# One norm inside a fused four-block kernel: held weight parts, reordered tile work, and row sums moved from TensorE to GpSimd

## The reference, cut to what matters

```
h = h + rms_norm(mlp_out, norm_ffn_post)            # first model, its last step
sh_m, sc_m, g_m, sh_f, sc_f, g_f = split(silu(c) @ ada_w + ada_b, 6)
h = rms_norm(x, mix_norm) * (1 + sc_m) + sh_m
u = h @ w_in                                        # 5 chunks of 512: a_b, a_c, a_x, r_gate, r_x
y_a = a_b * conv(a_c * a_x);  xr = conv(r_x) + b
y_b = gelu(r_gate) * rg_lru(xr)                     # two gates from xr, then a scan
x = x + g_m * (concat(y_a, y_b) @ w_out)
hf = rms_norm(x, ffn_norm) * (1 + sc_f) + sh_f      # then the SwiGLU, times g_f
```

## Time and profile before

| | |
|---|---|
| Median of 3 runs | 873.94 us (873.6 to 875.2) |
| The profiled execution's own time | 873.45 us |
| Its span, first to last instruction | 871.6 us |
| TensorE busy | 865.7 us, 99% of the span |
| VectorE, ScalarE, GpSimd busy | 714.4, 492.2, 102.3 us |
| Norm and entry in the chain (from the last down matmul to the first of unit U_WIN+2) | 293.37 to 309.93 us |

### The profile page before, as it was taken

One profiled execution on the slowest core, in us unless ns is written; L12 is line 12 of the kernel. 1 busy time (PEld: TensorE's weight loads), 2 busy tenths in 40 slices (PEclk: granted clock), 3 DMA queues, 4 the chain that ended last, 5 costly groups with the idle time before them and its releaser, 6 DMA issues.

```text
span 871.6 us, 13244 instructions
## 1 busy us (share of the span) xinstructions
PE 865.7 (99%) x4801; PEld 739.4 (85%) x4801; DVE 714.4 (82%) x740; ACT 492.2 (56%) x670; POOL 102.3 (12%) x68
## 2 busy tenths in 40 slices
PE   9999999999999999999999999999999999999998
PEld 6998878888888799988888888878777988888887
DVE  6699989898998987998989899787897866655656
ACT  5545665555555757765555455555676555545542
POOL 6000100021120003017010411003000001100000
PEclk9999999999999999999999999999999999999999
DMA  7988669898899385547989798636434376666662
GB/s 253 346 283 315 209 221 333 334 360 331 324 345 340 114 274 186 182 139 216 398 306 333 259 359 298 195 121 216 142 102 152 124 228 182 187 195 189 191 194 72
DMA packets 117252, 208.07 MB, mean 239 GB/s; under 512 B 7259, under 2 KB 81355, under 8 KB 112086
## 3 DMA queue, kind: packets, MB, share of 16 engines
q1 hardware_dynamic: 116710, 205.31, 69.2%
q10 hardware_dynamic: 304, 2.10, 0.7%
q0 software_dynamic: 192, 0.05, 0.0%
HBM read 206.39 MB, written 1.05 MB: 238 GB/s over the span
## 4 chain that ended last, share of the span: by engine, by line
PE 94%; DVE 3%; ACT 1%; DMA 1%; issue 0%; POOL 0%; DVEq 0%; POOLq 0%
PE tp L2033 11%; PE ub L2033 11%; PE acc L1887 8%; PE acc L1890 8%; PE acc L1892 7%; PE tp L2035 6%; PE ub L2035 6%; PE acc L1848 5%; PE acc L1852 5%; PE acc L1851 5%; PE acc L2019 3%; PE acc L2021 3%; PE acc L2020 3%; DVE w_lo L1203 1%; PE tp L2100 1%; PE acc L2100 1%
## 5 line engine op out<-in xcount | busy, mean ns | idle before, releaser
L1203 DVE TENSOR_TENSOR w_lo<-w_raw,w_hi 128x1024 fp32r<-128x1024 f32 x270 | 342.7, 1286 | 77.3 <-ACT w_hi L758 76.8
L758 ACT ACTIVATE w_hi<-w_raw 128x1024 fp32r<-128x1024 f32 x270 | 282.6, 1056 | 196.6 <-PE acc L1892 45.8
L2033 PE MATMUL tp<-aT,w_hi 128*128 128x512 f32 x432 | 135.9, 396 | 0.0
L2033 PE MATMUL ub<-aT,w_hi 128*128 128x512 f32 x432 | 135.4, 395 | 0.0
L1887 PE MATMUL acc<-w_hi,hT_hi 128*128 128x512 f32 x266 | 103.8, 390 | 0.1
L1890 PE MATMUL acc<-w_lo,hT_hi 128*128 128x512 f32 x266 | 103.6, 390 | 0.0
L1892 PE MATMUL acc<-w_hi,hT_lo 128*128 128x512 f32 x262 | 102.0, 389 | 0.0
L2035 PEld LDWEIGHTS tp<-aT,w_lo 128*128 128x128 f32 x432 | 81.1, 188 | 19.2
L2035 PEld LDWEIGHTS ub<-aT,w_lo 128*128 128x128 f32 x432 | 81.1, 188 | 18.9
L666 POOL PARTITION_ALL_REDUCE mod<-mod x14 | 56.4, 4028 | 262.4 <-PE tp L2035 118.7
L2035 PE MATMUL tp<-aT,w_lo 128*128 128x256 f32 x432 | 84.9, 278 | 0.0
(11 more groups left out here) (341 smaller groups left out, 1422.1 us busy)
## 6 DMA issues: line engine op xcount, KB each, us to landing
ada_raw<-in_l_ada_w SPq DMA_DIRECT2D x24, 1024.0 KB, 6.5
w_raw<-in_l_ffn_w_gate SPq DMA_DIRECT2D x44, 512.0 KB, 4.6
w_raw<-in_l_ffn_w_up SPq DMA_DIRECT2D x44, 512.0 KB, 4.4
w_raw<-in_l_ffn_w_down SPq DMA_DIRECT2D x44, 512.0 KB, 3.7
w_raw<-in_w_up SPq DMA_DIRECT2D x32, 512.0 KB, 4.8
w_raw<-in_w_down SPq DMA_DIRECT2D x32, 512.0 KB, 5.6
scratch<-in_l_ada_w SPq DMA_DIRECT2D x14, 1024.0 KB, 7.5
w_raw<-in_attn_w_qkv SPq DMA_DIRECT2D x24, 512.0 KB, 7.3
```

The source lines that it names most:

```text
L758: act.activation(rounded_part(v), w_raw[:, v % SLOTS, :], ACT.Copy).then_inc(hi_done, 1)
L1203: dve.tensor_tensor(rest_part(v), w_raw[:, v % SLOTS, :], rounded_part(v).bitcast(F32), ALU.subtract).then_inc(lo_done, 1)
L2033: pe.matmul(banks[f], rounded_part(v)[:, c[f]], aT[:, :, b, :], start=b == 0, stop=False)
```

## The change

Of the down projection's last parts M0, M1 and M2 go to homes in `hold` and M3 to the upper half of `aT`; before, only M1 lay apart. Therefore token tile 1 of all four is left over until tile 0 is complete (`down_last` with `left=(0, 1)`). The chain of tile 1 goes first on VectorE (its residual ahead of tile 0's remainder), its transposes get banks of their own, and W2 and W3 are rounded by ScalarE earlier, between the squares of tile 0. The four sums by TensorE and the four copies by ScalarE go away; GpSimd now makes six reduces while the recurrent block begins, each released by the remainder of a part (W3, W7, twice W9, twice W13). The loads of two gains move ahead of the MLP's loop.

```diff
-        apart = {2 * (U_WIN - 2) + 1: (flat(aT_hi[:, 4:KB, :]), flat(aT_lo[:, 4:KB, :]))}
+        MLP_END = 2 * (U_WIN - 2)
+        apart = {MLP_END + 3: (flat(aT_hi[:, 4:KB, :]), flat(aT_lo[:, 4:KB, :]))}
...
+        held.update({MLP_END + n: n for n in range(3)})
...
-            if k == 2:
-                return [tp[:, 0, :], tp[:, 1, :]]
+            if k == 2 and t:
+                return [ub[:, 1, :], acc[:, 2, :]]
...
             mlp_slice(1)
+            sp.wait_ge(xn_done, 8)
+            sp.wait_ge(mix_used, 16)
+            load_gain(4)
+            load_gain(5)
             with sp.Fori(0, (NJ_MLP - 2) // 2) as i:
...
             pool.wait_ge(ada_used, 22)
-            partition_sums(G_F, G_F, w_used, parts_to(U_WIN + 5), 2)
+
+            def sum_behind(u, row, n):
+
+                c = row[:, n * CH:(n + 1) * CH]
+                partition_sums(c, c, lo_done, hi_count(2 * u + 1), 0)
+
+            sum_behind(U_WIN + 1, GATE_M, 0)
+            sum_behind(U_WIN + 3, G_F, 0)
+            sum_behind(U_WIN + 4, GATE_M, 1)
+            sum_behind(U_WIN + 4, SH_F, 0)
+            sum_behind(U_WIN + 6, G_F, 1)
+            sum_behind(U_WIN + 6, SH_F, 1)
...
                 half_rstd(0, 1, 5)
+                split_part(2 * u + 2)
                 act.wait_ge(x_half, 3)
...
                 half_rstd(0, 1, 6)
+                split_part(2 * u + 3)
+                act.wait_ge(post_scaled, 5)
+                half_square(1, 0, acc[:, 2, :], sq_half)
                 act.wait_ge(w_used, parts_to(u))
-                half_square(1, 1, acc[:, 3, :], sq_half)
-                act.wait_ge(post_scaled, 5)
-                half_square(1, 0, acc[:, 2, :], sq_done)
-                half_rstd(1, 0, 7)
+                half_square(1, 1, acc[:, 3, :], sq_done)
+                half_rstd(1, 1, 7)
                 norm_hi(2, 0)
-                split_part(2 * u + 2)
-                split_part(2 * u + 3)
...
-                ada_parts(4, 6)
                 norm_hi(2, 1)
-                ada_parts(6, 8)
...
-                dve.wait_ge(sq_half, 7)
+                dve.wait_ge(sq_done, n_rstd[0] + 1)
                 scaled(1, 1, g_post).then_inc(post_scaled, 1)
+                residual(1)
                 norm_lo(0, 0)
-                residual(1)
-                norm_lo(0, 1)
                 dve.wait_ge(norm_scaled, 2)
                 norm_rows(1, g, shift)
+                norm_lo(0, 1)
...
-                    ada_gain(0, 4, pool_sum, 6)
+                    ada_gain(0, 4, pool_sum, 9)
...
-            down(U_WIN - 2, 0, operand=last_h, left=(1,))
-            down(U_WIN - 1, 1, final=True, operand=last_h, left=(1,))
-            pe.wait_ge(ada_used, 22)
-            pe.wait_ge(post_scaled, 4)
-            ada_sums(4, 6)
-
-            entry(U_WIN, (acc[:, 0, :], acc[:, 1, :]), lambda: ada_sums(6, 7), lambda: ada_sums(7, 8), tile1_out=1)
+            down(U_WIN - 2, 0, operand=last_h, left=(0, 1))
+            down_last(U_WIN - 1, 1, operand=last_h)
+            win_entry(U_WIN, (acc[:, 0, :], acc[:, 1, :]))
```

More of the change, by code:

```diff
@@ L766, in home_free @@
                         act.wait_ge(pT_ready if held[v] == 3 else o_ready, HEADS)
+                elif v < U_WIN * 2:
+                    act.wait_ge(ada_used, 19 + held[v])
                 elif v < U_SG0 * 2:
@@ L1970, in down, with down_last @@
                         last.then_inc(w_used, 1)
-            def down_last(u, h, lo_count, between):
+            def down_last(u, h, lo_count=0, between=None, operand=(hT_hi, hT_lo)):
                 parts = [(2 * u + k - 2, 2 * (1 - h) + k) for k in range(2)] + [(2 * u + k, 2 * h + k) for k in range(2)]
@@ L1978, in down_last @@
                     for v, k in parts[2:]:
-                        down_block(v, k, 0, n, False, False, lo=False)
-                    if n == 0:
+                        down_block(v, k, 0, n, False, False, lo=False, operand=operand)
+                    if n == 0 and lo_count:
                         pe.wait_ge(hT_lo_done, lo_count)
                     for v, k in parts[2:]:
-                        last = pe.matmul(acc[:, n, :], hT_lo[:, k, 0:P], rounded_part(v)[:, n * CH:(n + 1) * CH],
+                        last = pe.matmul(acc[:, n, :], operand[1][:, k, 0:P], rounded_part(v)[:, n * CH:(n + 1) * CH],
                                          start=False, stop=v == parts[3][0])
@@ L1987, in down_last @@
                     for v, k in parts:
-                        last = down_block(v, k, 1, n, False, v == parts[3][0],
+                        last = down_block(v, k, 1, n, False, v == parts[3][0], operand=operand,
                                           between=between if n == 1 and v == parts[3][0] else None)
@@ L2075, in entry, with rounded @@
-                pe.wait_ge(n_lo, 4 * k + 4)
-                for p in range(2, 4):
-                    part_ready(2 * u + p)
-                    products(0, p, aT_hi, rest_part, end=p == 3)
-                    products(1, p, aT_hi, rest_part)
-                    products(1, p, aT_lo, rounded_part, end=p == 3).then_inc(w_used, 1)
+                def rounded(t, p):
+                    pe.wait_ge(n_hi, 4 * k + 2 * t + 1 + p // 2)
+                    pe.wait_ge(hi_done, hi_count(2 * u + p))
+                    return products(t, p, aT_hi, rounded_part, begin=p == 0)
@@ new lines, in operand_rest, with weight_rest @@
+                def operand_rest(t, p):
+                    pe.wait_ge(n_lo, 4 * k + 2 * t + 1 + p // 2)
+                    return products(t, p, aT_lo, rounded_part)
+                def weight_rest(t, p):
+                    part_ready(2 * u + p)
+                    return products(t, p, aT_hi, rest_part, end=p == 3)
+                pe.wait_ge(post_scaled, 4)
+                norm_T(k, 0)
+                for p in range(2):
+                    rounded(0, p)
+                for p in range(2):
+                    weight_rest(0, p)
@@ new lines, in win_entry @@
+                for p in range(2, 4):
+                    rounded(0, p)
+                for p in range(2):
+                    operand_rest(0, p)
+                norm_T(k, 1)
+                for p in range(2, 4):
+                    operand_rest(0, p)
+                for p in range(4):
+                    rounded(1, p)
+                for p in range(2):
+                    weight_rest(1, p)
+                for p in range(2):
+                    operand_rest(1, p).then_inc(w_used, 1)
@@ L2082, in norm_begun @@
+                for p in range(2, 4):
+                    operand_rest(1, p)
+                for p in range(2, 4):
+                    weight_rest(0, p)
+                    weight_rest(1, p).then_inc(w_used, 1)
             def norm_begun(k):
@@ L2389, in _ @@
             tp_banks = tp[:, 0, :], tp[:, 1, :]
-            def ada_sums(n0, n1):
-                for n in range(n0, n1):
-                    pe.matmul(sum_bank(n), ones[:, :], mod[:, n * CH:(n + 1) * CH], start=True,
-                              stop=True).then_inc(ada_sum, 1)
             mlp_entry(U_MLP, tp_banks)
```

62 lines of the change are left out of this document (15 added, 47 removed).

## The result

The changed kernel takes 875.86 us (median of 22 executions, 874.32 to 878.27) against 873.99 of the kernel before (873.31 to 875.20, 22 executions): a ratio of 1.0024, with a 95% interval from 1.0018 to 1.0029. It is slower by 1.9 us, where 873.1 and no measurable change were forecast, and it lies outside the range (871.5 to 875.2). The profiled execution took 875.69 us, with a span of 873.9.

A forecast was written before the change was run, and what follows sets the result against it. TensorE was taken as the bound, busy 99% of the span. Norm -1.88 plus G0 +1.24 gave -0.64: 872.8 from the profiled execution, 873.3 from the median; forecast 873.1, range 871.5 to 875.2.

The forecast's parts named there:

- The norm: Down projection's end to the entry's end: ends at 308.05 against 309.93, a gain of 1.88 us, bounded by 1.2 and 2.2.
- the idle ahead of them: Sign at the norm: TensorE idle 1.5 to 1.8 us between tile 0's transposes and first product, ended by ScalarE's operand rounding.
- What was taken at nothing: Terms set at 0: down projection's new order, gains' loads, ScalarE's four copies (some 0.6 each, off the path), some reduces.
- The gains' loads: 1 MB moved into the MLP's full-DMA stretch, landings 2.6 us later: taken as 0, at worst 1 us; costing-case chance 0.04.
- the fifth and sixth reduce: Behind W13: M7 and a 4.03 us wait take most; D0 0.9 late, W14 to W17 have more in hand: 0.
- The place and the mechanism of the loss: Reduces delay VectorE at convolution C0, 3.2 us late against slack 1.96, so first gate product G0 loses 1.24 us.
- its four TENSOR_SCALAR read one SBUF operand and I take them as free: At C0's start: the four run beside the reduces unheld and end at 319.3.
- the second reduce: Behind W7: its hold goes to 315.7 while W8 would start at 315.4, costing 0.3 us.
- the third: First reduce behind W9: holds to 320.2 after the TENSOR_SCALARs end at 319.3, costing C0 0.85 us.
- the fourth: Other reduce behind W9, 3.2 us after the one before: stops C0's twelve small instructions in their middle, costing 2.05 us.
- The length of a hold: VectorE beside a reduce: held until 2.1 us after its start, 1.1 before its recorded end; 0 to 2.1 us per reduce.
- The slower rival: At C0: reduces block for all they last, 6.6 us less 1.96 gives 4.7 at G0, 876.3 total; chance 0.09.

The follow-up runs named there:

- experiment 3: Changed kernel with GATE_M and SH_F not summed at all and G_F's two reduces placed as before the change (other output): 871.65 us, ratio 0.9980 to the kernel before.
- experiment 5: Changed kernel with no reduce behind W9: one GATE_M half summed in the MLP, the other behind W17: 871.56 us, ratio 0.9975 to the kernel before.
- experiment 7: The kernel of experiment 5 with the two gains' loads back behind the down projection's last slice: 877.30 us, ratio 1.0039 to the kernel before.
- experiment 8: The changed kernel itself run once more, nothing altered: 875.86 us, ratio 1.0022 to the kernel before.
- experiments 4: Kernel before the change with G_F's two reduces waiting for W9's remainder, so both fall on C0: 877.76 us, ratio 1.0042.
- experiment 9: Kernel before with C0's four TENSOR_SCALARs made four times and G_F's two reduces one unit later, none beside C0: 876.66 us, ratio 1.0037.
- experiments 6: Kernel before with C0's four TENSOR_SCALARs made four times, reduces left where they were: 879.77 us, ratio 1.0067.
- experiment 1: Changed kernel with two reduces (GATE_M's halves) moved into the MLP's last slice, none behind W9: 873.75 us, ratio 0.9999 to the kernel before.
- experiment 2: Changed kernel with GATE_M's first half summed in the MLP and only its second half behind W9: 873.02 us, ratio 0.9991 to the kernel before.

## Why the prediction was wrong

**The norm: right.** 1.88 us were forecast. The chain gives 2.21 between two profiled executions, 2.03 of it in the norm itself, and the kernel with the norm alone 1.9 in the medians. Two inner terms were off and cancel in part. Tile 0's products start at 295.24 where 296.1 was worked out, so the idle ahead of them is 0.69 us and not the 1.5 to 1.8 that were named as a sign. The sixteen take 4.20 in place of 3.64; among them the weight loads wait 0.40 us for VectorE's remainder (L1218), which now stands behind tile 1's residual, a wait that the prediction doesn't have.

**What was taken at nothing: right.** The gains' loads, the copies, the down projection's order and the fifth and sixth reduce cost nothing that can be told: the first three are in experiment 3, the two reduces in experiment 5. What the text did not see is that the loads' new place is needed (experiment 7).

**The place and the mechanism of the loss: right.** C0 is held by the two reduces behind W9, and G0 waits for it.

**Its size: the step that failed is "its four TENSOR_SCALAR read one SBUF operand and I take them as free".** They are held as the others are: 3.79 to 3.82 us for 1.37, in three kernels. By terms, C0 ends later against the norm's end by 0.35 for the second reduce (2.70 for 2.35; 0.3 forecast), 2.42 for the third (0.85 forecast) and 1.86 for the fourth (2.05 forecast): 4.63 where 3.2 was forecast. That is exactly what the trace shows: from the norm's end to C0's end 328.36 - 307.72 = 20.64, where it was 325.94 - 309.93 = 16.01. Less the slack of 1.96 this gives a wait of 2.67; the row has 2.65, and 1.24 was forecast. The third term's 1.57 makes up the difference, and the fourth gave 0.19 back. The length of a hold was right: the held TENSOR_SCALAR starts at 317.9 and ends 2.33 later, so without its own 0.40 the hold reached to some 2.1 us behind the reduce's start (317.78), as read from the earlier trace rows. What was wrong is which instructions it stops, and that a second, short one comes near the reduce's end. The slower rival was to be decided by 3.8 us of delay at G0. The delay from the handover alone is 2.81 and stays under it; with the lower clock behind it (1.69) it is 4.50 in the profiled execution. The rival's own picture (6.6 us, each reduce blocking for all it lasts) was not what came: one reduce costs 1.9 to 2.4 us, also among small instructions.

The Trainium skill tells of this term. Its page "SBUF — State Buffer", section "SBUF: two separate sides", names not only VectorE's instructions with two inputs in SBUF, but also those in a performance mode that uses two ports. Its page "VectorE: DVE Perf Modes", section "The perf-mode tier table (the rule you actually need)", lists tensor_scalar on fp32 in SBUF at twice the plain rate, which by the same section needs both read ports. No row here shows in which mode the four ran. The trace agrees as far as the holding goes (2326 ns for 400), and disagrees with a hold "for the whole instruction": the two groups of C0 lost 2.42 and 1.86 us to reduces of about 3.3, and between its two losses one TENSOR_SCALAR took its plain 0.40 (at 320.2) with the reduce still on record, as far as GpSimd's recorded times can be trusted.

**Left out altogether: what a wait does to TensorE's clock.** It was no term of the sum. In 22 of 33 executions of the changed kernel the mean granted clock is 0.998 or less, and these are 1.5 us longer than the others (876.13 against 874.66 in experiment 8). Two of the 22 have a trace, and in both the clock is at its lower level for a few us behind the wait at G0 and nowhere else in the span; for the other 20 that is inferred. With the full clock throughout, the kernel takes 875.1 (the median of the eight such executions among the first 22), just inside the range and 1.1 us over the kernel before. Of the miss of 2.8 us, 0.8 is this term (875.86 less 875.09) and 1.4 the wait that was sized too small (2.65 for 1.24). Neither alone, added to the 873.1, would have left the range. Of the 0.6 that are left, 0.25 is the starting point: 873.1 lies 0.89 under the 873.99 that the kernel before took beside the changed one, where the sum was 0.64. The rest can't be told from the uncertainty of the medians.

Put together: -1.9 for the norm (medians), +2.8 from the norm's end to G0 (the traces), and 1.5 for the clock in two of three executions. That gives +0.9 at the full clock, where 1.0 and 1.1 were measured, and +2.4 else, where 2.5 and 2.6 were measured. The median lies between, nearer to the second: 1.9 and 2.2.

What stays open: what decides between two executions of one kernel whether the clock falls. The waits of TensorE for one handover line up with it (none of 11 executions at 0.80 us, 5 of 11 in experiments 4 and 9 at 2.33 and 2.30, 22 of 33 at 2.65, all 10 in experiments 6 and 7 at 4.16 and 3.27). One execution of experiment 1, whose longest wait there is 0.90 us, has 0.998 too and no trace. These kernels differ in other ways too, and no run varied the wait alone over more than two lengths.

## What to carry to other kernels

Work that is moved to an idle engine is not free if its instructions hold up another engine's: put each such instruction where the other engine waits anyway, one at a time, and check the slack of that very handover. Here three of the six reduces cost VectorE 4.6 us where they stood. Spread so that none falls on C0, one in the MLP and one behind W17, the six cost the path nothing that can be told; with two in the MLP they cost some 2 us again. When an estimate says that a dense TensorE will get a new wait, count the wait and beside it what the half clock behind it may cost, here 1.5 us.

## What the runs showed of the hardware

- A PARTITION_ALL_REDUCE of 128x512 fp32 on GpSimd delays one VectorE instruction in its way by 1.86 to 1.93 us at C0: a SCALAR_TENSOR_TENSOR from 0.48 to 2.335, a TENSOR_SCALAR with a single tensor input from 0.40 to 2.326. Near its end it holds a TENSOR_SCALAR once more, from 0.40 to 0.895 (0.893 with one reduce alone, experiment 2), so that the group lost 2.42 us. The twelve SCALAR_TENSOR_TENSORs ran on to the end of the other reduce and lost 1.86 with no second hold.
- It goes the other way too: the reduce lasts 3.25 us alone (303.79) and 5.25 where it starts at 311.21, into a VectorE instruction of 2.34 us that began at 311.03. So its recorded time seems to hold its own wait for the other instruction's end (313.37).
- TensorE's granted clock went from 1.00 to 0.50 behind waits of 2.3 to 4.2 us in a kernel whose TensorE is busy for 99% of the span, in some executions and not in others (five traces have it: 2.33, 2.65, 2.68, 3.27 and 4.16; that of experiment 9 has 2.30 and the full clock). The eight gate products and what stands up to the second matmul behind them took 3.53 us with the clock at its lower level for most of it, and 332.17 - 330.25 = 1.92 at the higher one (experiment 9, behind a wait of 2.30): 1.6 us.
